# Another order of the weight slabs, and other places for the small work, in a fused retention and attention block

## The chip, the cores and the metric

The kernel runs on one core of one Trainium2 chip. The metric is the device time of one execution in microseconds (us): the median of three runs is 1175.92 us (1172.63 to 1175.97).

## The reference

One layer of a streaming encoder for 256 tokens of width 2048. The change touches only the last line, the feed-forward part, and the edge to the output projection ahead of it:

```
h = rms_norm(x, norm1_g)
rq, rk, rv, rg, aq, ak, av = split(h @ w_in)
x = x + concat(silu(rg) * group_norm(retention(rq, rk, rv)), chunk_attention(aq, ak, av)) @ w_out
h = rms_norm(x, norm2_g)
x = x + square(relu(h @ w_ff1)) @ w_ff2        # 2048 -> 8192 -> 2048
```

## The kernel before

Every float32 product is made of three matmuls of rounded operands: high by high, high by low, low by high. A weight slab of 512 rows and 512 columns (128 x 2048 in the memory, 1 MB) is loaded into one of five buffers `raw`; ScalarE rounds it into `w_hi` (`hi_slab`, L904), VectorE writes the remainder into `w_lo` (`lo_slab`, L1244), and TensorE multiplies with both. `w_hi` and `w_lo` hold three slabs: ScalarE may begin on slab s when TensorE has done slab s-3.

The projections and the heads come first. The output projection's last column block and the whole feed-forward part are one sequence of 16 pairs p of column blocks, kinds U U D D (two pairs of the up product, two of the down product) four times. Half of each pair's product is done by a seven-product scheme on 2 x 2 blocks (products Q1, P5, P6, Q2, P7, P3, P4, 12 matmuls each), the other half plainly (R1 to R4, 24 matmuls each). The R slabs that stand in the sequence at pair p belong to pair p-1, so the loop's body p works on the rests of `prev` = p-1 and the products of p. The order of the 11 slabs of a pair is one tuple, `R1, Q1, R2, P5, R3, P6, R4, Q2, P7, P3, P4 = range(STEPS)`. TensorE, ScalarE and VectorE each have a program written by hand over it, and each works strictly in its own order.

Slabs for P5 and P6 are sums of raw slabs that VectorE makes in place (`sum_slabs`, L1252: a+b, then a+d); those for P7 and P4 are made by DMAs of GpSimd that add a slab onto a buffer (L453 and L457, `add_slabs`), started when VectorE's sum, and P6's `w_lo`, are done. SyncE issues the plain loads in a fixed order, each when `w_lo` of the buffer's last reader is written; `raw_plan` works that out.

The left operands of the down product come from the up product: output sums in `hid` (`up_sum`, L1330), `relu` (L943), `square` (L948), transposes on TensorE (`hid_blocks`, L672), copies `stage` into `sd` (L960), differences `d_mix_of` (L1374), then `d_hi` (L963) and `d_lo` (L1370) into eleven forms `dF_hi`, `dF_lo`. Products share banks: `keep_q1` (L955) and `sum_u1`, `sum_u3`, `sum_u2`, `sum_v4` (L1354, L1358, L1362, L1366) take Q1, P6, P5 and P7 out of `bankC` and `bankD`. The down product's results go to the residual stream `xs` by `add_products` (L1338) and `add_bank` (L1348).

Of the kernel before, what the change touches and what calls it, by code (L numbers as in the profile page):

```python
# [56 lines left out]
R1, Q1, R2, P5, R3, P6, R4, Q2, P7, P3, P4 = range(STEPS)  # L57
# [7 lines left out]
def hybrid_block(nc, x, x_cols, w_att, w_ret, w_out, w_up, w_down, gains, rel_windows, rope_cos, rope_sin, decay, out):  # L65
# [3 lines left out]
    with ExitStack() as ctx:  # L69
# [288 lines left out]
        def _(sp):  # L358
# [54 lines left out]
            for c in range(4):  # L413
                for m in range(MT):

                    sp.wait_ge(acc_read_dve, added(PAIRS - 2 + c // 2) + 2 * (c % 2) + m + 1)
                    sp.dma_start(out_rows[:, m, c * N:(c + 1) * N], xs[:, m, c * N:(c + 1) * N]).then_inc(stored, 16)
# [53 lines left out]
        def _(pe):  # L471
# [148 lines left out]
            def rest(p, step, hi, lo, form, banks, opens, closes):  # L620
# [4 lines left out]
                for m in range(MT):  # L625
# [49 lines left out]
            for p in range(PAIRS + 1):  # L675
# [6 lines left out]
                def forms(n):  # L682

                    if up:
                        pe.wait_ge(hF_lo_ok, n)
                    else:
                        pe.wait_ge(dF_lo_ok, FORMS * g + n)
# [9 lines left out]
                else:  # L697
                    rest_forms(9)
                    rest(p, R1, hi_, lo_, REST, (bH, bY), (False, False), False)
                if live:  # L700
                    forms(1)
# [9 lines left out]
                if live:  # L711
                    forms(3)
# [8 lines left out]
                if live:  # L721
                    forms(6)
# [8 lines left out]
                if live:  # L731
                    forms(7)
                    bank_read(pe, prev, 0)
                    product(p, Q2, hi, lo, A12, bH, False)
                    pe.wait_ge(u1_ok, p + 1)
                    product(p, P7, hi, lo, S3N, bX, True)
                    bank_read(pe, prev, 2)
                    product(p, P3, hi, lo, S4, bZ, False)
                    if was_up:
                        hid_blocks(prev, 1)  # L740
                    if prev < 0:
                        x_blocks(OUT_GROUPS - 1)
                    bank_read(pe, prev, 1)
# [4 lines left out]
        def _(act):  # L748
# [201 lines left out]
            def keep_q1(p):  # L950

                act.wait_ge(slab_used, slab_no(p, Q1) + 1)
                if p > 0:
                    bank_read(act, p - 1, 0)
                nc.scalar.activation(q1[:], bX[:], ACT.Copy).then_inc(q1_ok, 1)  # L955

            def stage(u, n):

                act.wait_ge(hid_tr, 8 * (u // 4) + n + 1)
                nc.scalar.activation(sd[:, n, :], bT[n % 2][:], ACT.Copy).then_inc(d_stage, 1)  # L960
# [8 lines left out]
            for p in range(PAIRS + 1):  # L969
                prev, s = p - 1, STEPS * p  # L970
                was_up, first_up, live = kind(prev) == "U", prev >= 0 and prev % 4 == 0, p < PAIRS
                if not live:
# [7 lines left out]
                if prev % 4 == 1 and prev >= 0:  # L980
                    act.wait_ge(d_mix, 4 * (prev // 4) + 2)
                    d_hi(S1, sd[:, 1, :])
                    d_hi(A12, sd[:, 2, :])
                    d_hi(A22, sd[:, 3, :])

                hi_slab(s + 3)
                if prev % 4 == 1 and prev >= 0:
                    act.wait_ge(d_mix, 4 * (prev // 4) + 3)
                    d_hi(S2N, sd[:, 0, :])
# [5 lines left out]
                if prev % 4 == 1 and prev >= 0:  # L995
                    act.wait_ge(d_mix, 4 * (prev // 4) + 4)
                    d_hi(S4, sd[:, 2, :])

                hi_slab(s + 5)
                keep_q1(p)  # L1000

                hi_slab(s + 6)
                if was_up:
# [5 lines left out]

                hi_slab(s + 7)  # L1010

                hi_slab(s + 8)
                if first_up:
                    stage(prev, 0)
# [5 lines left out]
                hi_slab(s + 9)  # L1020
                if was_up:
                    relu(prev, 0, 1)
                    relu(prev, 1, 1)
                    square(prev, 0, 1)
                    square(prev, 1, 1)
                if first_up:
                    d_hi(A11, sd[:, 0, :])

                hi_slab(s + 10)
                if p == 0:  # L1030
                    stream_squares(OUT_GROUPS - 1)
                if first_up:
                    act.wait_ge(d_mix, 4 * (prev // 4) + 1)
                    d_hi(S3N, sd4[:])

                hi_slab(s + 11)

                hi_slab(s + 12)
                if first_up:
                    stage(prev, 2)  # L1040
                    stage(prev, 3)
                elif was_up:
                    d_rest(prev, 2)
                    d_rest(prev, 3)
# [3 lines left out]
        def _(dve):  # L1048
# [283 lines left out]
            def add_products(p, m, second):  # L1332
# [4 lines left out]
                dve.wait_ge(ready, p + 1)  # L1337
                nc.vector.tensor_tensor(cols, other[:], cols, ALU.add).then_inc(xs_ok, 1)  # L1338

            def add_bank(p, m, second):  # L1340
# [4 lines left out]
                if p >= 0:  # L1345
                    dve.wait_ge(xs_ok, added(p) - 2 * OUT_GROUPS + 2 * second + m + 1)
# [28 lines left out]

            for p in range(PAIRS + 1):
                prev, s = p - 1, STEPS * p
                kept, live = kind(prev), p < PAIRS
                first_up = prev >= 0 and prev % 4 == 0
                second_up = prev >= 0 and prev % 4 == 1  # L1380
                g = prev // 4
                if not live:
# [4 lines left out]
                    for second in range(2):  # L1387
                        for m in range(MT):
                            add_products(prev, m, second)
                    for second in range(2):  # L1390
                        for m in range(MT):
                            add_bank(prev, m, second)
# [4 lines left out]
                else:  # L1397
                    sum_u2(prev)
# [5 lines left out]
                if second_up:  # L1404
                    dve.wait_ge(d_stage, 4 * g + 4)
                    d_mix_of(sd[:, 1, :], sd[:, 1, :], sd[:, 3, :], ALU.subtract)
                    d_lo(g, 3, S1, sd[:, 1, :])

                lo_slab(s + 3)
                if p > 0:  # L1410
                    sum_v4(prev)
                if second_up:
                    d_lo(g, 4, A12, sd[:, 2, :])
                    d_lo(g, 5, A22, sd[:, 3, :])
                    dve.wait_ge(d_mix, 4 * g + 2)
                    d_mix_of(sd[:, 0, :], sd[:, 1, :], sd[:, 0, :], ALU.subtract)

                sum_slabs(p, "a", "d", ["d"])
                lo_slab(s + 4)
                if p == 0:  # L1420
                    x_stage_rest(OUT_GROUPS - 2)
                    x_rest(OUT_GROUPS - 2)
                if second_up:
                    d_lo(g, 6, S2N, sd[:, 0, :])
                    dve.wait_ge(d_mix, 4 * g + 3)
                    d_mix_of(sd[:, 2, :], sd[:, 2, :], sd[:, 0, :], ALU.add)
                if kept == "D":
                    add_products(prev, 0, 0)
                    add_products(prev, 1, 0)

                lo_slab(s + 5)
                if second_up:
                    d_lo(g, 7, S4, sd[:, 2, :])
                if kept == "U":
                    up_sum(prev, 0, 0)
                    up_sum(prev, 1, 0)
                if kept == "D":
                    add_bank(prev, 0, 0)
                    add_bank(prev, 1, 0)

                lo_slab(s + 6)

                lo_slab(s + 7)

                if kept == "D":
                    add_products(prev, 0, 1)
                    add_products(prev, 1, 1)
                sum_u1(p)
                lo_slab(s + 8)
                if kept == "U":  # L1450
                    up_sum(prev, 0, 1)
                else:
                    add_bank(prev, 0, 1)

                lo_slab(s + 9)
                if kept == "U":
                    up_sum(prev, 1, 1)
                else:
                    add_bank(prev, 1, 1)
                if first_up:  # L1460
                    d_lo(g, 1, A11, sd[:, 0, :])
                    d_mix_of(sd4[:], sd[:, 0, :], sd[:, 1, :], ALU.subtract)
                if second_up:
                    d_lo(g, 8, REST, bT[0][:])
                    d_lo(g, 9, REST + 1, bT[1][:])

                lo_slab(s + 10)
                if first_up:
                    d_lo(g, 2, S3N, sd4[:])

                lo_slab(s + 11)
                sum_u3(p)
# [4 lines left out]
                if second_up:  # L1477
                    d_lo(g, 10, REST + 2, bT[0][:])
# [61 lines left out]
```

## Time and profile before

| | |
|---|---|
| median of three runs | 1175.92 us |
| the profiled execution | 1176.99 us |
| its span, first to last instruction | 1175.0 us |
| mean granted TensorE clock | 0.988 of full speed |
| TensorE (matmul) busy | 1124.2 us, 96% |
| VectorE busy | 888.5 us, 76% |
| ScalarE busy | 632.8 us, 54% |
| DMA read rate over the span | 215 GB/s |

Busy time is the time in which an instruction was running on the engine. Idle time of an engine is put down to what it waited for last. The granted clock is the share of full speed that TensorE was given. The 16 pairs fill the span's second part: pair 1 begins at 463.60 us, and the sequence of the last pair's products ends at 1149.51 us.

### The profile page before, as it was taken

What the parts mean: (1) busy time and instruction counts of PE and PEld (TensorE: products, weight loads), DVE (VectorE), ACT (ScalarE), POOL (GpSimd) and SP (SyncE); (2) the same over time, 40 slices, a digit from 0 to 9 for tenths busy, and PEclk for the clock granted to TensorE, in tenths of its full rate; (3) what the DMA queues carried; (4) which work ended last, traced back from release to release, by engine and by line L of the source; (5) the groups of instructions that cost most, each with busy time, mean ns of one, the idle gap of its engine ahead of it and who ended that gap; (6) DMA issues with size and microseconds to landing.
All of it is one profiled execution on the core that took longest, in us unless ns stands there. A gap on an engine that the chain in (4) does not pass through costs nothing.

```text
span 1175.0 us, 13700 instructions
## 1 busy us (share of the span) xinstructions
PE 1124.2 (96%) x5234; PEld 948.8 (81%) x5234; DVE 888.5 (76%) x924; ACT 632.8 (54%) x717; POOL 53.4 (5%) x58
## 2 busy tenths in 40 slices
PE   8999999999999999988999998999998999997998
PEld 8889889989988878776788876788876788876787
DVE  6667667657657678786898877888876889877885
ACT  6545445445454556556555555555565554574652
POOL 0000000000000000100000000000000000000000
PEclk9999999999999999999999998999999999999999
DMA  9745445445455467866688765688866788875692
GB/s 358 303 165 195 161 169 191 166 148 207 165 195 180 179 215 250 231 198 214 193 266 282 228 218 183 213 281 248 238 232 166 224 294 230 265 238 139 232 259 100
DMA packets 39551, 253.14 MB, mean 215 GB/s; under 512 B 4432, under 2 KB 4944, under 8 KB 12624
## 3 DMA queue, kind: packets, MB, share of 16 engines
q1 hardware_dynamic: 34896, 218.93, 50.7%
q0 software_dynamic: 4608, 33.56, 15.4%
q8 instruction: 33, 0.54, 0.2%
q14 instruction: 14, 0.11, 0.0%
HBM read 250.37 MB, written 2.10 MB: 215 GB/s over the span
## 4 chain that ended last, share of the span: by engine, by line
PE 75%; DVE 11%; ACT 8%; issue 3%; DMA 2%; SPq 0%; ACTq 0%; DVEq 0%
PE acc L485 10%; PE acc L487 10%; PE acc L486 10%; PE acc L628 8%; PE acc L631 8%; PE acc L630 8%; DVE w_lo L1244 6%; ACT w_hi L904 5%; PE bankC L614 2%; PE bankC L616 2%; PE bankC L615 2%; PE acc L614 2%; PE acc L616 2%; PE acc L615 2%; DMA raw<-in_w_ret 1%
## 5 line engine op out<-in xcount | busy, mean ns | idle before, releaser
L1244 DVE TENSOR_TENSOR w_lo<-raw,w_hi 128x2048 fp32r<-128x2048 f32 x180 | 411.4, 2288 | 120.9 <-ACT w_hi L904 120.9
L904 ACT ACTIVATE w_hi<-raw 128x2048 fp32r<-128x2048 f32 x180 | 342.3, 1912 | 193.7 <-PE acc L631 120.2
L1051 DVE TENSOR_TENSOR w_lo<-raw,w_hi 128x1024 fp32r<-128x1024 f32 (+1 forms) x152 | 167.6, 1107 | 67.1 <-ACT w_hi L756 67.0
L485 PE MATMUL acc<-w_hi,hT_hi 128*128 128x512 f32 (+1 forms) x512 | 191.6, 374 | 2.9 <-DVE w_lo L1051 2.9
L487 PE MATMUL acc<-w_hi,hT_lo 128*128 128x512 f32 (+1 forms) x512 | 185.7, 363 | 0.0
L486 PE MATMUL acc<-w_lo,hT_hi 128*128 128x512 f32 (+1 forms) x512 | 185.5, 362 | 0.0
L756 ACT ACTIVATE w_hi<-raw 128x1024 fp32r<-128x1024 f32 (+1 forms) x152 | 142.8, 963 | 33.8 <-PE acc L487 27.5
L628 PE MATMUL acc<-w_hi,hF_hi 128*128 128x512 f32 x256 | 103.6, 405 | 15.3 <-DVE w_lo L1244 14.3
L485 PEld LDWEIGHTS acc<-w_hi,hT_hi 128*128 128x128 f32 x512 | 96.3, 188 | 13.2 <-DVE w_lo L1051 3.8
L487 PEld LDWEIGHTS acc<-w_hi,hT_lo 128*128 128x128 f32 x512 | 96.1, 188 | 10.2
L486 PEld LDWEIGHTS acc<-w_lo,hT_hi 128*128 128x128 f32 x512 | 96.4, 188 | 9.5
L631 PE MATMUL acc<-w_hi,hF_lo 128*128 128x512 f32 x256 | 101.9, 398 | 0.0
L630 PE MATMUL acc<-w_lo,hF_hi 128*128 128x512 f32 x256 | 101.6, 397 | 0.0
L628 PE MATMUL acc<-w_hi,dF_hi 128*128 128x512 f32 x256 | 100.0, 391 | 0.1
L630 PE MATMUL acc<-w_lo,dF_hi 128*128 128x512 f32 x256 | 99.7, 390 | 0.0
L631 PE MATMUL acc<-w_hi,dF_lo 128*128 128x512 f32 x256 | 99.6, 389 | 0.0
L1252 DVE TENSOR_TENSOR raw<-raw 128x2048 f32<-128x2048 f32 x32 | 73.0, 2282 | 0.0
L628 PEld LDWEIGHTS acc<-w_hi,hF_hi 128*128 128x128 f32 x256 | 49.5, 193 | 27.8 <-issue 16.5
L631 PEld LDWEIGHTS acc<-w_hi,hF_lo 128*128 128x128 f32 x256 | 49.2, 192 | 10.8
L630 PEld LDWEIGHTS acc<-w_lo,hF_hi 128*128 128x128 f32 x256 | 49.7, 194 | 10.1
L628 PEld LDWEIGHTS acc<-w_hi,dF_hi 128*128 128x128 f32 x256 | 48.2, 188 | 10.9 <-issue 0.9
L631 PEld LDWEIGHTS acc<-w_hi,dF_lo 128*128 128x128 f32 x256 | 48.2, 188 | 10.1
(191 smaller groups left out, 1716.4 us busy)
## 6 DMA issues: line engine op xcount, KB each, us to landing
raw<-in_w_up SPq DMA_DIRECT2D x64, 1024.0 KB, 6.1
raw<-in_w_down SPq DMA_DIRECT2D x64, 1024.0 KB, 5.0
raw<-in_w_ret SPq DMA_DIRECT2D x32, 1024.0 KB, 4.8
raw<-in_w_att SPq DMA_DIRECT2D x28, 768.0 KB, 4.3
raw<-in_w_out SPq DMA_DIRECT2D x16, 1024.0 KB, 4.9
raw<-in_w_up POOLq DMA_DIRECT2D x16, 1024.0 KB, 8.6
raw<-in_w_down POOLq DMA_DIRECT2D x16, 1024.0 KB, 8.8
raw<-in_w_att SPq DMA_DIRECT2D x8, 384.0 KB, 7.2
```

Source lines behind the costliest of these rows:

```text
L485: nc.tensor.matmul(o, hi[:, k, tile_cols(m)], wh, start=first, stop=False)
L486: nc.tensor.matmul(o, hi[:, k, tile_cols(m)], wl, start=False, stop=False)
L487: mm = nc.tensor.matmul(o, lo[:, k, tile_cols(m)], wh, start=False, stop=last)
L614: nc.tensor.matmul(bank[:], hi[:, form, tile_cols(t)], wh[:, cols], start=t == 0, stop=False)
L628: nc.tensor.matmul(banks[m][:], hi[:, form + m, tile_cols(t)], wh[:, cols], start=opens[m] and t == 0, stop=False)
L630: nc.tensor.matmul(banks[m][:], hi[:, form + m, tile_cols(t)], wl[:, cols], start=False, stop=False)
L631: mm = nc.tensor.matmul(banks[m][:], lo[:, form + m, tile_cols(t)], wh[:, cols], start=False, stop=closes and t == SLAB_KT - 1)
L756: nc.scalar.activation(piece(w_hi, q, 0, PIECE_KT * n), raw[:, q // 2, (q % 2) * PIECE_KT * n:(q % 2 + 1) * PIECE_KT * n], ACT.Copy).then_ ...
L904: nc.scalar.activation(w_hi[:, ring(s)], raw[:, r, :], ACT.Copy).then_inc(slab_hi, 1)
L1051: nc.vector.tensor_tensor(piece(w_lo, q, 0, PIECE_KT * n), raw[:, q // 2, (q % 2) * PIECE_KT * n:(q % 2 + 1) * PIECE_KT * n], piece(w_hi, ...
L1244: nc.vector.tensor_tensor(w_lo[:, ring(s)], raw[:, r, :], w_hi[:, ring(s)].bitcast(f32), ALU.subtract).then_inc(slab_lo, 1)
L1252: nc.vector.tensor_tensor(raw[:, r, :], raw[:, r, :], raw[:, q, :], ALU.add).then_inc(summed, 1)
```

## The change

The tuple of the order becomes `R1, Q1, R2, P5, Q2, R3, P6, R4, P7, P3, P4`: Q2 goes from behind R4 to behind P5. So the products in a row are Q1 alone, P5 Q2, P6 alone, and P7 P3 P4; before they were four, Q2 P7 P3 P4.

The small work moves with it:

- The loads: Q2's own slab (`e`) is loaded ahead of `d`, and the buffers turn over otherwise. R3's slab, which was loaded when R1's `w_lo` was done, is now loaded when R2's is; R4's was loaded after R2's and is now after Q2's.
- TensorE: the second transposes of an up pair (`hid_blocks(prev, 1)`), which stood between P3 and P4, go into the next pair, between the two halves of R1.
- VectorE: `sum_u3` goes from near the end of a pair to the next one's start, ahead of `sum_u2`; `sum_v4` one slab earlier; both first output sums (`read_first`) directly behind Q2's `w_lo`, ahead of R3's; in a down pair the banks are added ahead of the products. The forms come in the order A11, A12, S1, S2N, S3N, S4, A22, and A12 to A22 beside the slabs of the pair after.
- ScalarE: `keep_q1` goes two slabs later, `relu` and `square` behind R4's and the next R1's and Q1's slab, and A11 and A12 are rounded from the bank directly.
- The wait conditions follow; the first two output stores of each column pair wait on `xs_ok`.

```
-R1, Q1, R2, P5, R3, P6, R4, Q2, P7, P3, P4 = range(STEPS)
+R1, Q1, R2, P5, Q2, R3, P6, R4, P7, P3, P4 = range(STEPS)
@@ sources
-                order += [(p, "d")] if p < PAIRS else []
+                order += [(p, "e"), (p, "d")] if p < PAIRS else []
                 order += [(p - 1, "R3"), (p - 1, "R4")]
-                order += [(p, "e")] if p < PAIRS else []
@@ TensorE
+                    rest(p, R1, hi_, lo_, REST, (bH, bY), (False, False), False,
+                         (lambda: hid_blocks(p - 2, 1)) if kind(p - 2) == "U" else None)
...
+                    forms(Q2)
+                    bank_read(pe, prev, 0)
+                    product(p, Q2, hi, lo, A12, bH, False)
...
-                    if was_up:
-                        hid_blocks(prev, 1)
@@ VectorE
+            def read_first(p):
+
+                for m in range(MT):
+                    up_sum(p, m, 0) if kind(p) == "U" else add_bank(p, m, 0)
...
+                    sum_u3(prev)
                     sum_u2(prev)
                 sum_slabs(p, "a", "b", ["b"])
                 lo_slab(s + 2)
+                if p > 0:
+                    sum_v4(prev)
...
                 sum_slabs(p, "a", "d", ["d"])
                 lo_slab(s + 4)
+                if p > 0:
+                    read_first(prev)
+
+                lo_slab(s + 5)
```

In the rows below, which are read from the programs and not from a trace, a name in brackets is the semaphore waited for. First VectorE in the third pair of a group (its operand forms are made there), from ahead of the first slab sum to R3's `w_lo`. Before:

```order
L1362 TENSOR_TENSOR u_59<-bankC,u_59 128x512 [waits slab_used]
L1252 TENSOR_TENSOR raw<-raw 128x2048 [waits raw_in1]
L1244 TENSOR_TENSOR w_lo<-raw,w_hi 128x2048 [waits slab_hi]
L1374 TENSOR_TENSOR sd<-sd 128x512 [waits d_stage]
L1370 TENSOR_TENSOR dF_lo<-sd,dF_hi 128x512 [waits dF_hi_ok]
L1244 TENSOR_TENSOR w_lo<-raw,w_hi 128x2048 [waits slab_hi]
L1366 TENSOR_TENSOR v_61<-bankD,u_59 128x512 [waits u2_ok]
L1370 TENSOR_TENSOR dF_lo<-sd,dF_hi 128x512 [waits dF_hi_ok] x2
L1374 TENSOR_TENSOR sd<-sd 128x512 [waits d_mix]
L1252 TENSOR_TENSOR raw<-raw 128x2048 [waits raw_in4]
L1244 TENSOR_TENSOR w_lo<-raw,w_hi 128x2048 [waits slab_hi]
```

The last row is R3's slab. Now, from the same place to Q2's slab, with the two output sums and R3's slab behind it:

```order
L1269 TENSOR_TENSOR raw<-raw 128x2048 [waits raw_in1]
L1261 TENSOR_TENSOR w_lo<-raw,w_hi 128x2048 [waits slab_hi]
L1387 TENSOR_TENSOR v_61<-bankD,u_59 128x512 [waits u2_ok]
L1395 TENSOR_TENSOR sd_64<-sd 128x512 [waits d_stage]
L1391 TENSOR_TENSOR dF_lo<-sd,dF_hi 128x512 [waits dF_hi_ok]
L1261 TENSOR_TENSOR w_lo<-raw,w_hi 128x2048 [waits slab_hi]
L1391 TENSOR_TENSOR dF_lo<-sd_64,dF_hi 128x512 [waits dF_hi_ok]
L1395 TENSOR_TENSOR sd<-sd 128x512
L1269 TENSOR_TENSOR raw<-raw 128x2048 [waits raw_in4]
L1261 TENSOR_TENSOR w_lo<-raw,w_hi 128x2048 [waits slab_hi]
L1347 TENSOR_TENSOR hid<-acc,q_58 128x512 [waits q1_ok,hid_tr,half_used]
L1347 TENSOR_TENSOR hid<-acc,u_59 128x512 [waits u2_ok,hid_tr,slab_used]
```

One small operation fewer stands between the two slab sums, the slab behind the second sum is Q2's, and both sums of `hid` now stand ahead of R3's.

TensorE at the end of the third pair of a group, between P3 and P4, before:

```order
L616 MATMUL acc<-w_hi,dF_lo 128x512
L672 MATMUL bankA<-ident,hid 128x128 [waits dF_lo_ok,hid_ok]
L672 MATMUL bankA<-ident,hid 128x128 x3
L672 MATMUL bankB<-ident,hid 128x128 [waits dF_lo_ok,hid_ok]
L672 MATMUL bankB<-ident,hid 128x128 x3
L614 MATMUL acc<-w_hi,dF_hi 128x512 [waits slab_lo,up_ok]
```

and the same transposes now, inside R1 of the next pair:

```order
L639 MATMUL acc<-w_hi,dF_lo 128x512
L682 MATMUL bankA<-ident,hid 128x128 [waits dF_lo_ok,hid_ok]
L682 MATMUL bankA<-ident,hid 128x128 x3
L682 MATMUL bankB<-ident,hid 128x128 [waits dF_lo_ok,hid_ok]
L682 MATMUL bankB<-ident,hid 128x128 x3
L636 MATMUL acc<-w_hi,dF_hi 128x512
```

The transposes no longer stand between two products.

## Rows read from the trace of the kernel before

**Rows 1.** Windows, pairs 1-15, 4, 5, 6, 7: length, engines busy, PEclk, DMA share, GB/s.
```profile
463.60:1149.51 685.91, 645.15 (x2829) 527.41 (x2828) 565.02 (x410) 387.56 (x306) 28.64 (x31) 0.98 0.74 229
605.82:646.62 40.80, 40.80 (x181) 33.78 (x180) 36.28 (x26) 21.60 (x12) 1.73 (x2) 1.00 0.83 259
646.62:691.97 45.35, 42.85 (x198) 35.33 (x196) 35.09 (x24) 28.61 (x26) 1.73 (x2) 1.00 0.73 225
691.97:746.82 54.85, 48.03 (x198) 38.29 (x198) 42.35 (x33) 30.16 (x29) 1.73 (x2) 0.91 0.65 204
746.82:787.65 40.83, 40.83 (x182) 33.78 (x180) 36.04 (x28) 21.59 (x12) 1.73 (x2) 1.00 0.79 248
```

**Rows 2.** Waits of PE in pairs 1 to 15: total us, times, longest.
```profile
PE acc L614 <- DVE w_lo L1244: 17.9, 8, 2.5
PE acc L628 <- DVE w_lo L1244: 14.3, 4, 3.7
```

**Rows 3.** Timeline of PE in pair 6: start, us, instruction [idle before <-releaser].
```profile
713.39 0.76 PE L628 MATMUL acc<-w_hi,hF_hi 128*128 128x512 f32 x1 [3.64 <-DVE w_lo L1244]
713.95 0.63 PE L630 MATMUL acc<-w_lo,hF_hi 128*128 128x512 f32 x1
714.38 0.63 PE L631 MATMUL acc<-w_hi,hF_lo 128*128 128x512 f32 x1
...
742.40 0.47 PE L614 MATMUL acc<-w_hi,dF_hi 128*128 128x512 f32 x1 [1.99 <-DVE w_lo L1244]
```

**Rows 4.** Timeline of ACT and DVE in pair 6, slabs P5 and R3.
```profile
700.24 1.68 ACT L963 ACTIVATE dF_hi<-sd 128x512 fp32r<-128x512 f32 x3 [6.10 <-DVE sd L1374]
...
703.75 2.29 DVE L1244 TENSOR_TENSOR w_lo<-raw,w_hi 128x2048 fp32r<-128x2048 f32 x1 [2.15 <-ACT w_hi L904]
...
710.95 2.29 DVE L1244 TENSOR_TENSOR w_lo<-raw,w_hi 128x2048 fp32r<-128x2048 f32 x1 [0.30 <-ACT w_hi L904]
```

**Rows 5.** Timeline of PE, transposes of pair 5.
```profile
671.11 0.60 PE L672 MATMUL bankA<-ident,hid 128*128 128x128 f32 x4
...
671.90 0.47 PE L628 MATMUL acc<-w_hi,hF_hi 128*128 128x512 f32 x1
672.21 0.39 PE L630 MATMUL acc<-w_lo,hF_hi 128*128 128x512 f32 x1
```

**Rows 6.** Timeline of pair 8, which begins at 787.65: DVE, POOL, SP, then ACT.
```profile
787.23 2.28 DVE L1244 TENSOR_TENSOR w_lo<-raw,w_hi 128x2048 fp32r<-128x2048 f32 x1
789.43 0.68 DVE L1362 TENSOR_TENSOR u<-bankC,u 128x512 f32<-128x512 f32 x1
790.03 2.28 DVE L1252 TENSOR_TENSOR raw<-raw 128x2048 f32<-128x2048 f32 x1
792.23 2.29 DVE L1244 TENSOR_TENSOR w_lo<-raw,w_hi 128x2048 fp32r<-128x2048 f32 x1
792.61 0.86 POOL L453 DMA_DIRECT2D raw<-in_w_up  x1 [26.25 <-DVE raw L1252]
794.54 0.33 SPq L411 DMA_DIRECT2D raw<-in_w_down  x1
...
793.35 1.92 ACT L904 ACTIVATE w_hi<-raw 128x2048 fp32r<-128x2048 f32 x1 [3.52 <-PE acc L631]
```

**Rows 7.** DMA issues at 794.54, 792.61, 786.74 and 975.08: size, us to landing.
```profile
raw<-in_w_down SPq DMA_DIRECT2D x1, 1024.0 KB, 8.5
...
raw<-in_w_up POOLq DMA_DIRECT2D x1, 1024.0 KB, 9.0
...
raw<-in_w_down SPq DMA_DIRECT2D x1, 1024.0 KB, 4.7
...
raw<-in_w_down SPq DMA_DIRECT2D x1, 1024.0 KB, 10.0
```

**Rows 8.** Timeline of DVE and PE in pair 1, ahead of R2.
```profile
471.48 1.29 DVE L1266 TENSOR_TENSOR hF_lo<-sx,hF_hi 128x512 fp32r<-128x512 f32 x2
...
472.82 0.50 PE L628 MATMUL acc<-w_hi,hF_hi 128*128 128x512 f32 x1 [0.91 <-DVE hF_lo L1266]
```

More of the change, by code:

```diff
@@ L414, in _ @@
                 for m in range(MT):
-                    sp.wait_ge(acc_read_dve, added(PAIRS - 2 + c // 2) + 2 * (c % 2) + m + 1)
+                    if c % 2 == 0:
+                        sp.wait_ge(xs_ok, products_added(PAIRS - 2 + c // 2) + m + 1)
+                    else:
+                        sp.wait_ge(acc_read_dve, added(PAIRS - 2 + c // 2) + 2 + m + 1)
                     sp.dma_start(out_rows[:, m, c * N:(c + 1) * N], xs[:, m, c * N:(c + 1) * N]).then_inc(stored, 16)
@@ L618, in product, with rest @@
                 mm.then_inc(slab_used, 1)
-            def rest(p, step, hi, lo, form, banks, opens, closes):
+            def rest(p, step, hi, lo, form, banks, opens, closes, between=None):
                 s = slab_no(p, step)
@@ L634, in rest @@
                         mm.then_inc(half_used, 1)
+                    if between and m == 0:
+                        between()
                 mm.then_inc(slab_used, 1)
@@ L698, in _ @@
                     rest_forms(9)
-                    rest(p, R1, hi_, lo_, REST, (bH, bY), (False, False), False)
+                    rest(p, R1, hi_, lo_, REST, (bH, bY), (False, False), False,
+                         (lambda: hid_blocks(p - 2, 1)) if kind(p - 2) == "U" else None)
                 if live:
-                    forms(1)
+                    forms(Q1)
                     if p > 0:
@@ L731, in _ @@
                 if live:
-                    forms(7)
-                    bank_read(pe, prev, 0)
-                    product(p, Q2, hi, lo, A12, bH, False)
+                    forms(P7)
                     pe.wait_ge(u1_ok, p + 1)
                     product(p, P7, hi, lo, S3N, bX, True)
+                    forms(P3)
                     bank_read(pe, prev, 2)
                     product(p, P3, hi, lo, S4, bZ, False)
-                    if was_up:
-                        hid_blocks(prev, 1)
                     if prev < 0:
                         x_blocks(OUT_GROUPS - 1)
+                    forms(P4)
                     bank_read(pe, prev, 1)
@@ L952, in keep_q1, with stage @@
                 act.wait_ge(slab_used, slab_no(p, Q1) + 1)
-                if p > 0:
+                if kind(p - 1) == "U":
                     bank_read(act, p - 1, 0)
+                elif kind(p - 1) == "D":
+                    act.wait_ge(xs_ok, products_added(p - 1) + 1)
                 nc.scalar.activation(q1[:], bX[:], ACT.Copy).then_inc(q1_ok, 1)
-            def stage(u, n):
+            def stage(u, n, form=None):
                 act.wait_ge(hid_tr, 8 * (u // 4) + n + 1)
+                if form is not None:
+                    d_hi(form, bT[n % 2][:])
                 nc.scalar.activation(sd[:, n, :], bT[n % 2][:], ACT.Copy).then_inc(d_stage, 1)
@@ L970, in _ @@
                 prev, s = p - 1, STEPS * p
-                was_up, first_up, live = kind(prev) == "U", prev >= 0 and prev % 4 == 0, p < PAIRS
-                if not live:
+                was_up = kind(prev) == "U"
+                fresh_first = prev >= 0 and prev % 4 == 0
+                held_first, held_second = p >= 2 and p % 4 == 2, p >= 2 and p % 4 == 3
+                g = (p - 2) // 4
+                if p == PAIRS:
                     for s in range(STEPS * PAIRS + 2, SLABS_ALL):
@@ L979, in _ @@
                     x_rest(OUT_GROUPS - 1)
[L980 to L984, printed above, removed]
+                if held_first:
+                    stage(p - 2, 2, A12)
+                    stage(p - 2, 3)
+                if held_second:
+                    d_rest(p - 2, 2)
+                    d_rest(p - 2, 3)
                 hi_slab(s + 3)
-                if prev % 4 == 1 and prev >= 0:
-                    act.wait_ge(d_mix, 4 * (prev // 4) + 3)
-                    d_hi(S2N, sd[:, 0, :])
+                if held_first:
+                    act.wait_ge(d_mix, 4 * g + 1)
+                    d_hi(S1, sd4[:])
                 hi_slab(s + 4)
@@ L994, in _ @@
                     stream_squares(OUT_GROUPS - 2)
-                if prev % 4 == 1 and prev >= 0:
-                    act.wait_ge(d_mix, 4 * (prev // 4) + 4)
-                    d_hi(S4, sd[:, 2, :])
                 hi_slab(s + 5)
+                hi_slab(s + 6)
+                if held_first:
+                    act.wait_ge(d_mix, 4 * g + 3)
+                    d_hi(S2N, sd[:, 0, :])
+                hi_slab(s + 7)
                 keep_q1(p)
-                hi_slab(s + 6)
                 if was_up:
@@ L1008, in _ @@
                     square(prev, 1, 0)
-                hi_slab(s + 7)
+                if held_first:
+                    d_hi(S3N, sd[:, 1, :])
                 hi_slab(s + 8)
-                if first_up:
-                    stage(prev, 0)
+                hi_slab(s + 9)
+                if held_first:
+                    act.wait_ge(d_mix, 4 * g + 4)
+                    d_hi(S4, sd[:, 2, :])
+                    d_hi(A22, sd[:, 3, :])
+                if fresh_first:
+                    stage(prev, 0, A11)
                     stage(prev, 1)
@@ L1337, in add_products @@
                 dve.wait_ge(ready, p + 1)
+                if not second:
+                    dve.wait_ge(acc_read_dve, added(p) + m + 1)
                 nc.vector.tensor_tensor(cols, other[:], cols, ALU.add).then_inc(xs_ok, 1)
@@ L1344, in add_bank @@
                 bank_done(p, m, second)
-                if p >= 0:
-                    dve.wait_ge(xs_ok, added(p) - 2 * OUT_GROUPS + 2 * second + m + 1)
+                if p >= 0 and second:
+                    dve.wait_ge(xs_ok, products_added(p) + 2 + m + 1)
                 bank = ((bH, bY), (bZ, bW))[second][m]
@@ L1353, in sum_u1 @@
                 dve.wait_ge(q1_ok, p + 1)
+                if kind(p - 1) == "D":
+                    dve.wait_ge(xs_ok, products_added(p - 1) + 2)
                 nc.vector.tensor_tensor(u1[:], bX[:], q1[:], ALU.add).then_inc(u1_ok, 1)
@@ L1374, in d_mix_of @@
                 nc.vector.tensor_tensor(dst, a, b, op).then_inc(d_mix, 1)
+            def read_first(p):
+                for m in range(MT):
+                    up_sum(p, m, 0) if kind(p) == "U" else add_bank(p, m, 0)
             for p in range(PAIRS + 1):
                 prev, s = p - 1, STEPS * p
[L1378 to L1382, printed above, removed]
+                was_up, was_down = kind(prev) == "U", kind(prev) == "D"
+                fresh_first, fresh_second = prev >= 0 and prev % 4 == 0, prev >= 0 and prev % 4 == 1
+                held_first, held_second = p >= 2 and p % 4 == 2, p >= 2 and p % 4 == 3
+                g = (p - 2) // 4
+                if p == PAIRS:
+                    sum_u3(prev)
                     sum_u2(prev)
@@ L1386, in _ @@
                     lo_slab(s + 3)
[L1387 to L1392, printed above, removed]
+                    read_first(prev)
+                    add_products(prev, 0, 0)
+                    add_products(prev, 1, 0)
+                    add_products(prev, 0, 1)
+                    add_products(prev, 1, 1)
+                    add_bank(prev, 0, 1)
+                    add_bank(prev, 1, 1)
                     break
@@ L1397, in _ @@
                 else:
+                    sum_u3(prev)
                     sum_u2(prev)
@@ L1403, in _ @@
                     stream_mean_squares()
-                if second_up:
+                if held_first:
                     dve.wait_ge(d_stage, 4 * g + 4)
-                    d_mix_of(sd[:, 1, :], sd[:, 1, :], sd[:, 3, :], ALU.subtract)
-                    d_lo(g, 3, S1, sd[:, 1, :])
-                lo_slab(s + 3)
[L1410 to L1416, printed above, removed]
+                    d_mix_of(sd4[:], sd[:, 1, :], sd[:, 3, :], ALU.subtract)
+                    d_lo(g, 2, A12, sd[:, 2, :])
@@ L1418, in _ @@
+                if held_second:
+                    d_lo(g, 10, REST + 2, bT[0][:])
+                    d_lo(g, 11, REST + 3, bT[1][:])
+                lo_slab(s + 3)
+                if held_first:
+                    d_lo(g, 3, S1, sd4[:])
+                    d_mix_of(sd[:, 1, :], sd[:, 0, :], sd[:, 1, :], ALU.subtract)
+                if p == 0:
+                    x_stage_rest(OUT_GROUPS - 2)
                 sum_slabs(p, "a", "d", ["d"])
                 lo_slab(s + 4)
+                if p > 0:
+                    read_first(prev)
@@ L1431, in _ @@
[L1431 to L1447, printed above, removed]
@@ L1463, in _ @@
-                if second_up:
-                    d_lo(g, 8, REST, bT[0][:])
-                    d_lo(g, 9, REST + 1, bT[1][:])
+                lo_slab(s + 8)
+                sum_u1(p)
+                lo_slab(s + 9)
+                for m in range(MT):
+                    up_sum(prev, m, 1) if was_up else add_bank(prev, m, 1)
+                if held_first:
+                    d_lo(g, 6, S4, sd[:, 2, :])
+                    d_lo(g, 7, A22, sd[:, 3, :])
+                if fresh_first:
+                    dve.wait_ge(d_stage, 4 * (prev // 4) + 1)
+                    d_lo(prev // 4, 1, A11, sd[:, 0, :])
@@ L1467, in _ @@
                 lo_slab(s + 10)
-                if first_up:
-                    d_lo(g, 2, S3N, sd4[:])
+                if fresh_second:
+                    d_lo(prev // 4, 8, REST, bT[0][:])
+                    d_lo(prev // 4, 9, REST + 1, bT[1][:])
                 lo_slab(s + 11)
-                sum_u3(p)
                 lo_slab(s + 12)
```

74 lines of the change are left out of this document (31 added, 43 removed).

## The prediction, written before the changed kernel ran

> **What bounds the kernel now.** I read the page first, then the stretches from one pair to the next, TensorE's waits, the timeline around the longest of them, and last the DMAs. TensorE sets the end: in an undisturbed pair (pair 4: 40.80 us long, 40.80 busy, clock 1.00) it never pauses [rows 1]. A pair is 180 matmuls, so one costs 0.2267 us, a product (12) 2.72 and a plain slab (24) 5.44. Pairs 4 and 7 take this time, pair 5 takes 45.35 and pair 6 54.85, where the clock is 0.91 and VectorE is busy 42.35 [rows 1]. So the loss sits in two of every four pairs. In the waits over pairs 1 to 15, all but about 9 us of TensorE's idle 40.8 (685.91 - 645.15) [rows 1] is for `w_lo`: 17.9 us in 8 waits at a product and 14.3 in 4 at a plain slab [rows 2].
>
> The timeline names the places. Eight times TensorE stands ahead of P4 (in pair 6 for 1.99 us), the last of four products in a row with transposes between; four times it stands ahead of R3 in the third pair of a group, for up to 3.7 (here 3.64) [rows 2, 3]. After the latter the starts of the matmuls are 0.43 us apart (713.95 to 714.38) instead of 0.23: the granted clock is the lower of its two levels, 1.2 GHz [rows 3]. The cause of the second: ScalarE's queue stood 6.10 us at a form that waited for VectorE's difference, with P5's slab behind it, and VectorE then waited 2.15 for that slab; its whole chain to R3 is late by this and by six small operations between the two slab sums [rows 4].
>
> **What the change can take away.** Pairs 1 to 15 without any loss are 15 x 40.80 = 612.0 plus 16 calls of the transposes. One call costs 0.79 (671.11 to 671.90) and 0.08 at the matmul behind it (0.31 to the next start instead of 0.23), 0.87 [rows 5]; 16 make 13.9. So 685.9 - 625.9 = 60.0 us are lost in these pairs, by waits and by the low clock behind them. The span without them is 1175.0 - 60.0 = 1115.0. The matmuls, slabs and small operations stay the same in number: nothing else is saved.
>
> **P4, part by part.** ScalarE begins on a slab 0.26 us after the slab three places ahead is done (R1 ends at 787.65 + 5.44 = 793.09, it starts at 793.35) and takes 1.92; VectorE, in a chain, needs 2.20 per slab or slab sum (787.23 to 789.43) and 0.60 per small operation (789.43 to 790.03) [rows 6]. TensorE starts 0.15 after `w_lo` ends (710.95 + 2.29 = 713.24, start 713.39) [rows 3, 4]. Ahead of P4 in the new order stand R4 (5.44), P7, P3. P4's rounding can begin when R4 is done, and VectorE has P7's and P3's slabs written by then, since R4 gives it 5.44 us. In the third pair, from R4's end: one output sum (0.6) and two form remainders, then P4's slab from 2.2 on, ready at 4.6 against 5.44. The wait ahead of P4 goes; next late would be R1's slab of the next pair, by my count 0.4 us in time. The transposes inside R1 cost TensorE the same 0.87 as before, with `hid` squared about 2 us earlier; beside R1's slab VectorE has none of them.
>
> **The third pair.** Counted from its start (pair 8's rows as the clock): Q1's `w_lo` ends at 1.78 (789.43 - 787.65) [rows 6]. Up to the first output sum VectorE then has 8 small operations (u3, u2, v4, two differences, remainders A12 and S1, the sum itself) and 5 large (two slab sums, slabs R2, P5, Q2): 4.8 + 11.0, so 17.6, and 0.08 + 0.15 to TensorE's start, 17.8. Q2 waits for this sum, since it opens the bank, and is due at 5.44 + 0.87 + 2.72 + 5.44 + 2.72 = 17.2: 0.6 late. R3's slab follows a second sum and is 0.1 later still. Then the load is light again. ScalarE's new waits for differences stand ahead of Q2's and R4's slabs, which have time to spare. So the third pair loses 0.7 instead of some 12 (54.85 - 40.80 - 2 x 0.87): 4 x 0.7 = 2.8.
>
> **What is new and costs.** R3's slab is now loaded when R2's `w_lo` is done. Before, the load in this place was R4's, which had another rest and product of time. In pair 8 R2's `w_lo` ends at 794.52, 6.87 after the start; SyncE issues at 794.54, 1.9 after GpSimd's adding DMA, and the load takes 8.5 to land [rows 6, 7]. Of the fifteen loads in this place thirteen take 8.4 to 8.6, one 7.6 and one 10.0; a load without that neighbour, at 786.74, takes 4.7 [rows 7]. `sum_u3` now stands ahead, +0.60, so: 6.87 + 0.60 + 0.02 + 8.5 = 16.0, ScalarE 0.05 + 1.92, VectorE 0.03 + 2.29, start + 0.15: 20.4. R3 is due at 5.44 + 2.72 + 5.44 + 2.72 + 2.72 = 19.04. This is a wait of 1.4 us in every first and second pair of a group (pairs 4, 5, 8, 9, 12, 13: 8.4), and 0.5 in the four fourth pairs, whose R1 holds the transposes (2.0); in the third the VectorE chain is as late. The price has no row of the new order. Its bounds: 4.7 to land gives no wait at all, 10.0 gives 2.9. I take 8.5, since the place, the neighbour and the 1.9 between them stay.
>
> The Trainium skill (DMA: Bandwidth & Descriptors, "Issuing engines are not separate DMA queues") says that transfers started by different engines end up on the same 16 DMA engines and interleave. The trace agrees in kind; two equal transfers sharing evenly would make 9.4 of the 4.7, where the row has 8.5. By that the wait would be 2.3, and the time some 11 us above mine.
>
> Pair 1: R2 waited 0.91 for `x`'s remainders, which were the last small work ahead [rows 8]; `sum_v4` now stands in front (+0.6) and ScalarE squares ahead of Q1's slab (+0.4 by my estimate, 0 to 1.2): 1.9, and 0.2 at R3. In pair 0 the load is early enough. The P4 sum's DMA starts behind P6's `w_lo`, at about 23; even 9.0 to land [rows 7] ends at 32, when its rounding may start (32.6 or later). The last stores wait for the same final sums: nothing.
>
> Sum: 2.8 + 8.4 + 2.0 + 2.1 = 15.3. Span 1115.0 + 15.3 = 1130.3. The profiled execution took 1.99 beyond its span, 1176.99, and the median of the runs is 1.07 below that: 1130.3 + 0.9 = 1131.2.
>
> **Rivals.**
> 1. R3's load is in time (it lands in less than 7.1). Then 10.4 of the 15.3 go: 1120.8. For it: a lone load takes 4.7. Against: thirteen of fifteen rows. 14%.
> 2. The wait at R3 is dearer: 10.0 to land (+1.5 in 14 pairs, 1152), or the clock falls to its lower level behind the short waits, at 13 matmuls x 0.20 = 2.6 each; in the six 1.4 waits that is +15.6, 1147. For it: after a wait of 1.99 at P4 the clock did fall [rows 3]. Against: those waits stood behind transposes, these stand behind a full product. 17%.
> 3. The change doesn't do what it says in the third pair: VectorE has the same twelve form operations there, and its queue and ScalarE's still wait for each other. If that pair stays at 54.85, 4 x 11.6 = 46 come back: about 1177, no change. For it: VectorE is busy 42.35 against TensorE's 42.5. Against: the row of 6.10 is caused by the place of one difference, which moves. 3%.
> 4. The other side, slower: one mechanism, R3's load, with the clock. Every pair waits 2.9 there (10.0 to land) and restarts at the lower clock, 2.6: 5.5 in 14 pairs is 77, so 1115 + 77 + 5 + 1 = 1198. It decides from 4.3 us per pair on (60 / 14). 2%.
>
> The forecast itself, 1124 to 1139, has 64%. The range of 1117 to 1152 takes in rivals 1 and 2. What this measurement can tell from no change is about 0.3%, 3.5 us. Faster by more than that: the forecast and rivals 1 and 2, 0.95; within it 0.03; slower 0.02.
>
> **What would show it.** Right: no waits at P4 of 2 us; third pairs of about 43.3; first pairs of 42.2 with a wait of 1.4 at R3, whose releaser chain is ScalarE's slab behind the DMA of `raw`; clock 1.00 in nearly every stretch. Wrong: R3 starting without a wait (rival 1), matmuls 0.43 apart in first pairs (rival 2), or third pairs above 50 (rival 3).

## The result and the profile after

The changed kernel took 1136.32 us (median of 4 runs, 1135.29 to 1140.22) against 1175.49: a ratio of 0.968, 95% interval 0.9659 to 0.9701. The forecast was 1131.2, with a range of 1117 to 1152. The profiled execution has a span of 1134.3 us, where the sum gave 1130.3.

Windows of the kernel after, from one pair's start to the next, to be read against [rows 1]: pairs 1 to 15 together, then 4, 5, 6, 7, 8, 12 and 14 (stretch, length, busy time of PE, PEld, DVE, ACT, POOL, granted clock, DMA share, GB/s).

```profile
462.84:1108.87 646.03, 633.15 (x2830) 519.69 (x2829) 564.06 (x410) 389.18 (x306) 28.57 (x31) 1.00 0.78 244
592.06:634.04 41.98, 41.06 (x181) 33.72 (x180) 36.36 (x26) 21.46 (x12) 1.72 (x2) 1.00 0.79 250
634.04:677.01 42.97, 42.00 (x190) 34.56 (x189) 34.58 (x23) 26.84 (x23) 1.72 (x2) 1.00 0.78 245
677.01:720.31 43.30, 42.98 (x197) 35.27 (x196) 40.92 (x34) 31.15 (x31) 1.72 (x2) 1.00 0.77 242
720.31:762.58 42.27, 42.10 (x190) 34.50 (x189) 37.72 (x28) 23.06 (x15) 1.73 (x2) 1.00 0.80 250
762.58:807.59 45.01, 42.68 (x182) 34.88 (x181) 36.37 (x26) 21.34 (x12) 1.72 (x2) 0.96 0.75 233
935.95:979.50 43.55, 41.04 (x181) 33.72 (x180) 36.36 (x26) 21.34 (x12) 1.73 (x2) 1.00 0.75 241
1022.54:1066.64 44.10, 43.15 (x197) 35.28 (x196) 40.93 (x34) 31.04 (x31) 1.73 (x2) 1.00 0.77 237
```

The pairs come in groups of four, so pair 4 is a first pair, 5 a second, 6 a third and 7 a fourth. The third pair went from 54.85 to 43.30 and the second from 45.35 to 42.97; the first became longer, 40.80 to 41.98. The lost time of pairs 1 to 15 fell from 60.0 to 646.0 - 625.9 = 20.1 us.

TensorE's waits in the same stretch, against [rows 2]: who, for what, total us, times, longest.

```profile
PE acc L636 <- DVE w_lo L1261: 9.3, 7, 2.5
PE acc L636 <- DVE hF_lo L1283: 1.7, 1, 1.7
PE acc L622 <- DVE hid L1347: 1.3, 4, 0.3
PE acc L636 <- DVE dF_lo L1391: 0.6, 4, 0.2
```

No wait is left ahead of P4. Seven waits, of 0.6 to 2.5, stand at a plain slab: R3 of pairs 4, 5, 8, 9, 12, 13 and 14. The `hid` row is Q2 in the third pairs, and the last row is R2 in the fourth.

The timeline of pair 4 (start, us, instruction [idle before <-releaser]) shows what R3 waits for. First ScalarE, then SyncE's issue and VectorE, then TensorE:

```profile
607.79 5.64 ACT L916 ACTIVATE w_hi<-raw 128x2048 fp32r<-128x2048 f32 x3 [5.40 <-DMA raw<-in_w_down]
...
599.47 7.53 SPq L416 DMA_DIRECT2D raw<-in_w_down  x2
...
606.56 1.29 DVE L1367 TENSOR_TENSOR xs<-acc,xs 128x512 f32<-128x512 f32 x2
609.74 2.29 DVE L1261 TENSOR_TENSOR w_lo<-raw,w_hi 128x2048 fp32r<-128x2048 f32 x1 [1.90 <-ACT w_hi L916]
...
612.18 0.47 PE L636 MATMUL acc<-w_hi,dF_hi 128*128 128x512 f32 x1 [0.92 <-DVE w_lo L1261]
```

The load is issued at 599.47, when R2's `w_lo` is done, and ScalarE stands 5.40 us until it has landed, at 607.8. VectorE is free and waits 1.90 for ScalarE. TensorE's wait is put down to `w_lo`; its origin is the DMA two steps back. The wait is 0.92 and the pair lost 41.98 - 40.80 = 1.18: what comes on top of a wait, some 0.26 here, is called the restart below.

Time to landing of that load in pairs 4, 8 and 12:

```profile
raw<-in_w_down SPq DMA_DIRECT2D x1, 1024.0 KB, 8.3
...
raw<-in_w_down SPq DMA_DIRECT2D x1, 1024.0 KB, 9.7
...
raw<-in_w_down SPq DMA_DIRECT2D x1, 1024.0 KB, 9.9
```

In pair 8 the wait at R3 is 2.33 and the clock falls 1.0 us after the restart: the spacing goes from 0.24 to 0.43.

```profile
784.11 0.47 PE L636 MATMUL acc<-w_hi,dF_hi 128*128 128x512 f32 x1 [2.33 <-DVE w_lo L1261]
...
784.88 0.40 PE L636 MATMUL acc<-w_hi,dF_hi 128*128 128x512 f32 x1
785.12 0.59 PE L638 MATMUL acc<-w_lo,dF_hi 128*128 128x512 f32 x1
785.50 0.63 PE L639 MATMUL acc<-w_hi,dF_lo 128*128 128x512 f32 x1
785.93 0.63 PE L636 MATMUL acc<-w_hi,dF_hi 128*128 128x512 f32 x1
```

### The profile page after: what moved, and what is told of

It reads as the page before. It is cut to its first block, busy times and chain, and to the rows that moved or that the text cites. A ratio compares the mean times of both kernels' runs of the same rounds, so it can differ in the third digit from the quotient of the medians.

```text
span 1134.3 us, 13704 instructions
## 1 busy us (share of the span) xinstructions
PE 1112.8 (98%) x5234; PEld 941.9 (83%) x5234; DVE 888.1 (78%) x924; ACT 634.3 (56%) x717; POOL 53.3 (5%) x58
## 4 chain that ended last, share of the span: by engine, by line
PE 68%; DVE 19%; DMA 7%; ACT 4%; issue 1%; SPq 0%; ACTq 0%
PE acc L493 10%; DVE w_lo L1261 10%; PE acc L495 10%; PE acc L494 10%; PE acc L636 7%; PE acc L639 6%; PE acc L638 6%; ACT w_hi L916 4%; DVE raw L1269 4%; DMA raw<-in_w_up 3%; DMA raw<-in_w_down 2%; PE bankC L624 2%; PE bankC L622 2%; PE bankC L623 2%; PE acc L622 2%; PE acc L624 2%
## 5 line engine op out<-in xcount | busy, mean ns | idle before, releaser
L638 PEld LDWEIGHTS acc<-w_lo,dF_hi 128*128 128x128 f32 x256 | 48.5, 189 | 9.5
```

The lines of the kernel that those rows point to most:

```text
L638: nc.tensor.matmul(banks[m][:], hi[:, form + m, tile_cols(t)], wl[:, cols], start=False, stop=False)
```

## The experiments

Two questions were put: does R3 wait for its load because of what stands beside it, and did the slab order or the placement of the small work bring the gain? The kernel before measured 1174.9 in both sets of runs, the first with e1 to e4, the second with e5 to e8.

**The adding DMA held back (e1).**

```
                 pool.wait_ge(summed, 2 * p + 1)
+                pool.wait_ge(slab_lo, slab_no(p, P5) + 1)
```

> The changed kernel, with GpSimd's adding DMA for P7's slab held back until P5's low slab is written (about 2.8 us behind the issue of R3's load instead of 1.9 ahead of it). Theory L (R3 waits for its load, which lands late beside the adding DMA): R3's load has the DMA engines to itself and lands in about 5 to 6.5 us instead of 8.3 to 9.8, the waits of 0.9 to 2.5 us at R3 in the first and second pairs go, 12 to 13 us in all: about 1123. Rival V (VectorE's chain up to R3's slab is the late one): no change, 1136. Rival M (the delay only moves the wait to R4's load or to P7's slab): 1130 to 1136 with new waits there.

Measured: 1127.51 us, ratio 0.9591 (0.9578 to 0.9604). The changed kernel had 1136.32 and 0.968, so this is 9 us faster; 13 were expected. R3's load, issued at 600.32, and R4's, issued at 607.53 behind the adding DMA's 603.63:

```profile
raw<-in_w_down SPq DMA_DIRECT2D x1, 1024.0 KB, 4.8
...
raw<-in_w_down SPq DMA_DIRECT2D x1, 1024.0 KB, 7.9
```

R3's wait went in every first and second pair. TensorE's three largest waits, then ScalarE and TensorE in pair 4:

```profile
PE bankC L623 <- issue: 2.3, 4, 1.0
PE acc L637 <- DVE hF_lo L1284: 1.7, 1, 1.7
PE acc L623 <- DVE hid L1348: 1.3, 4, 0.3
```

```profile
615.43 1.92 ACT L917 ACTIVATE w_hi<-raw 128x2048 fp32r<-128x2048 f32 x1 [4.01 <-DMA raw<-in_w_down]
617.25 0.58 ACT L970 ACTIVATE q<-bankC 128x512 f32<-128x512 f32 x1
...
617.92 0.47 PE L623 MATMUL bankC<-w_hi,hF_hi 128*128 128x512 f32 x1 [0.37 <-issue]
```

Theory L holds and V falls. M holds for a part: R4's load is now the slow one, and the copy of q1, which P6 needs, stands behind R4's slab in ScalarE's queue (4 waits, up to 1.0). The profile calls this "issue"; that it is the copy is read from the times: the copy ends at 617.25 + 0.58 = 617.83, and P6 starts at 617.92.

**The old slab order with the new placement (e2).** The tuple, the order of loads and the place of Q2 on TensorE as before; S2N's form, q1's copy and u1's sum one slab earlier.

```
-R1, Q1, R2, P5, Q2, R3, P6, R4, P7, P3, P4 = range(STEPS)
+R1, Q1, R2, P5, R3, P6, R4, Q2, P7, P3, P4 = range(STEPS)
```

> The changed kernel's placement of the small work, with the slab order of before (Q2 behind R4, four products in a row, R3's load released by R1's low slab again); S2N's form, q1's copy and u1's sum stand one slab earlier, as P6 does. Theory P (the placement of the small work brought the gain, the slab order only costs the wait at R3): no wait at R3, 1 to 2 us lost ahead of P4 and R1 in the third pairs, about 1126 to 1130. Rival O (at most three products in a row is what brought the gain): 1160 or more, with waits of 2 us or more ahead of P4 in the up pairs' bodies.

Measured: 1130.90, ratio 0.9626 (0.9613 to 0.9638), faster than the changed kernel with its new order. TensorE's waits:

```profile
PE acc L623 <- DVE dF_lo L1392: 3.0, 4, 0.8
PE acc L637 <- DVE hF_lo L1284: 1.7, 1, 1.7
PE acc L637 <- DVE w_lo L1262: 1.6, 4, 0.4
PE acc L623 <- DVE w_lo L1262: 1.3, 4, 0.3
```

Four products in a row cost one wait of 0.3 us at P4 in the second pairs and one of 0.75 at P3 in the third, for S4's remainder, and there is no wait at R3 for its load. The row of 1.6 is R1 at the start of the fourth pairs, behind VectorE's small operations. P holds, O falls: in the old order the placement is worth 1174.9 - 1130.9 = 44 us, and with it the new order costs 5 us (8 by the second measurement of the changed kernel, e5).

**The new slab order with the old placement (e3).** Tuple, loads and Q2's place as in the change; only the output sums stand ahead of R3's slab.

> The kernel before with the new slab order and its loads, but the small work where it was; only the output sums and stream adds ahead of Q2 stand one slab earlier, since Q2 opens their bank. Theory P: the eight waits ahead of P4 stay (2.0 to 2.5 us each), the third pair stays above 50 us, the wait of 1 to 1.5 us at R3 comes on top: 1170 to 1190. Rival O: the waits at P4 go, 1145 or less.

Measured: 1178.91, ratio 1.0034 (1.0021 to 1.0046): slightly slower than before. TensorE's waits:

```profile
PE acc L613 <- DVE hid L1330: 21.6, 4, 5.4
PE acc L613 <- DVE w_lo L1244: 6.6, 8, 1.1
PE acc L627 <- DVE w_lo L1244: 5.0, 7, 0.9
```

The order alone does shorten the eight waits of 2.0 to 2.5 at P4, to 1.1 in the second and 0.6 in the third pairs: the expectation that they stay was wrong. But Q2 needs the bank that VectorE reads for `hid`, and in the third pairs that sum is 5.4 us late. The total agrees with P.

**One edit on ScalarE in the kernel before (e4).** In the trace of before, ScalarE stood at the second relu of pair 5 with P4's slab (684.77) behind it. VectorE could write that slab's remainder only from 686.71, and TensorE started P4 at 689.14 after a wait of 2.50:

```profile
682.58 0.72 ACT L943 ACTIVATE hid<-hid,rstd 128x512 f32<-128x512 f32 x1 [2.35 <-DVE hid L1330]
...
684.77 1.90 ACT L904 ACTIVATE w_hi<-raw 128x2048 fp32r<-128x2048 f32 x1
```

```
-                if was_up:
-                    relu(prev, 0, 1)
...
+                hi_slab(s + 10)
+                if was_up:
+                    relu(prev, 0, 1)
+                    relu(prev, 1, 1)
+                    square(prev, 0, 1)
+                    square(prev, 1, 1)
```

> The kernel before, with one edit on ScalarE: the second relu and square of an up pair stand behind P4's slab instead of ahead of it. Theory Q (P4 was late in the kernel before because ScalarE's queue stood at a relu that waited for VectorE's sum, with P4's slab behind it): P4's slab is ready on time, the transposes wait about 1 us for the squares instead, 1 to 2 us saved in each of eight pairs: 1162 to 1170. Rival (four products in a row are too short for ScalarE and VectorE whatever the queue): 1174 to 1178.

Measured: 1155.21, ratio 0.9834 (0.9822 to 0.9847), 20 us faster than before, half of the change's gain. TensorE's waits:

```profile
PE acc L628 <- DVE w_lo L1245: 15.9, 8, 3.6
PE bankD L614 <- DVE v L1367: 3.7, 4, 0.9
PE bankA L672 <- ACT hid L948: 1.8, 4, 0.5
```

The row at L614 for `w_lo` [rows 2] is gone. The first row is R3, as before, at 3.6 in each third pair, with a wait of 0.3 at R2 in each fourth. Theory Q holds; its size was too low (9 us expected at the middle). The eight waits alone were 17.9 us, and the low clock behind three of them (507.32, 560.59 and 742.40 in the trace of before) goes too.

**Two edits on ScalarE (e7).** As e4, and in the third pair every rounding of a form one slab later.

```
                 hi_slab(s + 3)
+                if prev % 4 == 1 and prev >= 0:
+                    act.wait_ge(d_mix, 4 * (prev // 4) + 2)
+                    d_hi(S1, sd[:, 1, :])
+                    d_hi(A12, sd[:, 2, :])
+                    d_hi(A22, sd[:, 3, :])
```

> The kernel before with two edits on ScalarE alone: the second relu and square behind P4's slab, as in the one-edit kernel that measured 1155, and in the third pair every rounding of a form (S1, A12 and A22; S2N; S4) one slab later, behind R3's neighbours instead of ahead of them. Slab order, VectorE, TensorE and the loads are as before. Theory Q (the losses were ScalarE's queue standing at an instruction that waits for VectorE, with a slab behind it): the waits of 0.9 at P5 and 3.6 at R3 in the third pairs shrink to 1 to 1.5 together and the low clock behind them goes, 4 to 6 us in each of four: 1131 to 1140. Rival (the third pair is bound by VectorE's load of twelve form operations): 1150 to 1156.

Measured: 1135.12, ratio 0.9658 (0.9644 to 0.9672), level with the whole change. What stood at P5 and R3 is now one wait of 2.20 in each third pair (1 to 1.5 was expected). In pair 6 the spacing behind it stays at full speed:

```profile
696.29 0.47 PE L628 MATMUL acc<-w_hi,hF_hi 128*128 128x512 f32 x1 [2.20 <-DVE w_lo L1245]
696.60 0.40 PE L630 MATMUL acc<-w_lo,hF_hi 128*128 128x512 f32 x1
696.84 0.39 PE L631 MATMUL acc<-w_hi,hF_lo 128*128 128x512 f32 x1
```

In pairs 2 and 6 it does so; in pairs 10 and 14, after the same wait of 2.20, the clock fell, and these pairs are 46.8 us long instead of 45.8. Pair 10, 2.3 us behind its restart:

```profile
869.39 0.63 PE L631 MATMUL acc<-w_hi,hF_lo 128*128 128x512 f32 x1
869.82 0.63 PE L628 MATMUL acc<-w_hi,hF_hi 128*128 128x512 f32 x1
```

VectorE still has its twelve form operations in this pair, so they are not what cost the 12 us. But the 2.20 that are left are VectorE's own: R3's slab is rounded by 689.3, and VectorE, busy without a pause since 686.45, reaches it at 693.87.

```profile
687.37 1.91 ACT L904 ACTIVATE w_hi<-raw 128x2048 fp32r<-128x2048 f32 x1
...
693.87 2.28 DVE L1245 TENSOR_TENSOR w_lo<-raw,w_hi 128x2048 fp32r<-128x2048 f32 x1
```

So the rival (VectorE's load of small operations) holds for this rest.

**The changed kernel once more (e5).**

> The changed kernel, unchanged, profiled once more. In its first profile R3's load took 9.7 and 9.9 us in pairs 8 and 12 and 8.3 in the others. Theory F (fixed: the slabs of these pairs are slow to read): 9.7 or more again in pairs 8 and 12 and nowhere else. Theory C (chance: any of these loads can come about 1.5 us late in an execution): other pairs, or another number of them, and a time that differs from run to run by 2 to 5 us.

Measured: 1139.16 (1138.40 to 1140.34), ratio 0.9694. This is 2.8 us above the 1136.32 of the same kernel in the first measurement; differences of that size between the sets are not read as effects. R3's load in pairs 8 and 12 took 9.9 each:

```profile
raw<-in_w_down SPq DMA_DIRECT2D x1, 1024.0 KB, 9.9
```

Pair 14 had 9.5 in the first trace and 9.6 here; pair 10 had 8.5 there and 10.0 here; pair 1, whose load is issued ahead of the adding DMA, 5.9 and 5.8; all others 8.2 to 8.9. So both theories have a part: three pairs are slow in both traces, one came and went. The trace of e6 below has the same three, 9.6, 10.1 and 9.6 in pairs 8, 12 and 14. In those of e4 and e7, in the old order, the load at this place takes 8.5 to 8.7 in all three pairs; in that of before it was slow in pair 12 alone, the 10.0 of [rows 7]. What makes it slow stays open.

**The sum u3 back at the pair's end (e6).**

```
-                    sum_u3(prev)
                     sum_u2(prev)
...
                 lo_slab(s + 11)
+                sum_u3(p)
```

> The changed kernel with the sum u3 back at the end of a pair, behind R1's low slab, instead of at the next pair's start. Theory L (R3 waits for a load that R2's low slab releases): the release comes 0.5 us earlier, and the wait at R3 falls from about 0.9 to 0.4 us in the first and second pairs, 3 us in all: 1133. Rival (the landing is set by the adding DMA and not by the release): waits as before, 1136.

Measured: 1130.96 (1130.71 to 1135.06), ratio 0.9636 (0.9616 to 0.9656). R3 in pair 4 waits 0.47 where it waited 0.92:

```profile
611.17 0.47 PE L636 MATMUL acc<-w_hi,dF_hi 128*128 128x512 f32 x1 [0.47 <-DVE w_lo L1261]
```

and TensorE's waits in all:

```profile
PE acc L636 <- DVE w_lo L1261: 7.0, 7, 2.2
PE acc L636 <- DVE hF_lo L1283: 1.1, 1, 1.1
```

The wait follows the release, as theory L has it: it fell by 0.2 to 0.6 in each first and second pair. The gain was 5 us against the first measurement of the changed kernel and 8 against e5, and not 3. The row for `hid` is gone too, since the third pair's first sum was late by this one operation; the wait in pair 1 fell from 1.7 to 1.1; and behind the wait in pair 8, now 1.69, the clock stayed at full speed, which is worth 1.6. The expectation had none of these.

**A version that beats both (e8).** e1, with q1's copy behind P6's slab, and on VectorE:

```
                 lo_slab(s + 2)
+                if prev == 0:
+                    x_rest(OUT_GROUPS - 1)
+                if held_second:
+                    d_lo(g, 10, REST + 2, bT[0][:])
+                    d_lo(g, 11, REST + 3, bT[1][:])
                 if p > 0:
                     sum_v4(prev)
...
                 if held_first:
+                    d_mix_of(sd[:, 1, :], sd[:, 0, :], sd[:, 1, :], ALU.subtract)
                     dve.wait_ge(d_mix, 4 * g + 1)
```

> The changed kernel with P7's adding DMA held back until P5's low slab, as in the kernel that measured 1127.5, and four small moves: q1's copy one slab earlier on ScalarE (it stood behind R4's slab, whose load now lands later, and P6 waited 0.4 to 1.0 us for it); on VectorE the remainders of the rest forms, and of x's last block, ahead of v4's sum, and the difference for S3N behind the output sums. Expected: the waits at P6 go (2 us), those at R2 in the fourth pairs and at Q2 in the third pairs go or halve (2 to 4 us), R2 in the second pair 0.6 less: 1121 to 1124. If the waits only move on, 1126 to 1128.

Measured: 1122.33 (1121.19 to 1123.24), ratio 0.9549 (0.9536 to 0.9562). All of TensorE's waits from pair 1 on:

```profile
PE acc L637 <- DVE w_lo L1262: 1.6, 4, 0.4
PE acc L637 <- DVE hF_lo L1284: 1.1, 1, 1.1
PE acc L623 <- DVE dF_lo L1392: 0.3, 1, 0.3
```

3.0 us of waits are left. The span is 1121.3; the sum without any loss was 1115.0. The four moves were made together, so what each is worth is not shown.

## Why the prediction was right, step by step

The forecast of 1131.2 lies 5.1 us below the 1136.32 measured, and the measured time lies inside its range. One term of the sum was mis-sized, and two parts came out right with some luck.

- **The size of what could be gained, 60.0 us, and that TensorE sets the end:** right. The stretches after leave 20.1 of it, and e8, with a span of 1121.3 against 1175.0, shows that 54 can be had.
- **P4:** right that its wait goes, partly by luck. The reason given, the slack behind R4, is only a part of it: e3 has that slack alone, and waits of 1.1 and 0.6 are left. It is also not needed: e4 removes all eight waits in the old order, with four products in a row and the transposes between them. The waits came from ScalarE's queue, which stood at the second relu ahead of P4's slab. The changed kernel moves this relu behind P4's slab too; the list of the change does not say so, and the prediction did not count on it. The trace of before had the row (2.35 at the relu), but the prediction looked at ScalarE's queue in the third pair's first half only.
- **The third pair:** right, 0.7 forecast; 43.30 - 42.54 = 0.76 measured, with the wait at Q2 in the place that the chain gave (0.32, and what comes on top of it). The cause named, ScalarE's queue at a form, is borne out by e7; a rest of 2.20 is VectorE's own queue, which the prediction named beside it.
- **The first and second pairs:** the mechanism was right, and e1 and e6 show it: a load released by R2's `w_lo`, slow beside the adding DMA. 1.4 was forecast; pairs 4, 5, 9 and 13 lost 1.2 to 1.4, of which 0.9 to 1.0 is the wait itself. In pair 4 R3 starts at 612.18 - 592.06 = 20.1 after the pair's start, where the chain gave 20.4; the load took 8.3 instead of 8.5.
- **The mis-sized term** is this load's time in pairs 8, 12 and 14, 9.5 to 9.9 instead of 8.5. Pair 8 lost 45.01 - 40.80 = 4.2, of which the low clock is 1.6 (busy 42.68 against 41.04 in pair 12), pair 12 lost 2.8 and pair 14 lost 1.6, where 1.4, 1.4 and 0.7 stood in the sum. That is 5.1 us more; the whole sum, 15.3, fell short of the 20.1 by 4.8. The row of 10.0 [rows 7] had this; it was taken for a stray and used for the bound alone. Rival 2 was thus true for single pairs, with its long load in three and its low clock in one, at 1.6 and not 2.6. Its counter-argument, that the clock fell only behind transposes, does not hold: in pair 8 full products stand ahead of the wait, and in the trace of before the waits at R3 [rows 3] stood behind P5.
- **The fourth pairs:** the size was right (0.5 forecast, 0.6 in pair 7) and the place wrong, so this size is luck. They wait at R2, for the remainders of the rest forms, 0.16 and a restart; VectorE makes these behind v4's sum. The prediction never held that against R2's due time. R3 is then in time for the load.
- **Pair 1:** 1.7 of wait and the restart, 43.71 - 41.67 = 2.0 against 2.1 (506.55 - 462.84 is its length, 41.67 a pair with one call of the transposes). One reading was wrong, without effect: in the trace of before the load in this place took 5.9 in pair 1 (issued at 471.59, when R2's `w_lo` was done), and not 7.6.
- **Rival 1** (no wait at R3) is what e1 brings about, at 1127.5 instead of 1120.8. In its trace the waits at P6, from R4's load, make 2.3 of the difference, and the fourth pairs still lose about 0.6 each at R1 and R2, where the rival had nothing. **Rivals 3 and 4** did not come: the third pair loses 0.8 and not 12, and the short waits of 0.9 to 1.0 never pulled the clock down.

## What to carry to other kernels

When an engine waits, look at what stands in the queue of the engine that feeds it. An instruction that itself waits, with the needed work behind it, costs more than its own duration, and moving it by one place can be worth as much as a new schedule: 20 us by one edit here, 40 by two. When the order of work changes, list for each load which event now releases it, what else uses the DMA engines then, and how long such a load took in the trace; take the slow rows of that list as cases, not as strays.

## What the runs showed of the hardware that I had not expected

The load beside the adding DMA takes 8.2 to 8.9 us where one released 3.3 us ahead of that DMA takes 4.8 (e1, pair 4). In pairs 8, 12 and 14 it takes 9.5 to 10.1, in both traces of the changed kernel and in that of e6; why these pairs was not settled.

The length of a wait did not decide whether the clock fell behind it. In the changed kernel a wait of 2.33 us at R3 let it fall in pair 8, and one of 2.51 in pair 12 did not. In e7 four equal waits of 2.20 at R3 divide two and two. In the trace of before the clock stayed at full speed behind the wait of 3.67 in pair 14 (the matmuls start 0.23 apart from 1076.05 on), and fell behind P4's wait of 1.98 in pair 2.
